# A list of expert items made before a block barrier, and one tile's routing results made after it

## The chip, the cores and the metric

One NeuronCore of a Trainium2 chip runs the whole kernel; the metric is the device time of one execution in microseconds. Engines in the text: TensorE (PE), its weight loads (PEld), VectorE (DVE), ScalarE (ACT), GpSimd (POOL), SyncE (SP); a trailing q in a profile is an engine's sequencer or queue.

## What is computed

One layer of a hybrid block on 1024 tokens of width 1024, in float32: a normalised input goes through an mLSTM group and a differential-attention group, the two are joined, projected and added to the input, and a mixture of experts follows. Only its routing and its start matter here:

```python
u2 = rms_norm(h, norm2_g)
logits = u2 @ router_w + router_b
top_vals, top_idx = lax.top_k(logits, 4)          # 4 of 32 experts
gates = softmax(top_vals)
# tokens are gathered by expert, in blocks
gu = u2[tok] @ w_gu[e] + b_gu[e]
act = (clip(up) + 1) * gate * sigmoid(1.702 * gate)
h[tok] += (act @ w_down[e] + b_down[e]) * gates
out = rms_norm(h, final_g)
```

## The kernel before

`mix_and_route` (L1314) makes the output projection, the second norm and the routing, tile by tile: 8 tiles of 128 tokens, in pairs. `experts` (L1988) then works through a list of items. An item is one expert with up to 128 of its tokens, or up to 192 (two blocks); the list stands in `k.items`: expert, first slot and a flag for two blocks, 64 entries each, and at the end the count. Each of the two functions is one `nc.Block`, one program for each engine; at the end of a block all five engines meet at a barrier. Order within a block is written out by hand, with semaphores.

**Routing of a tile** on DVE (`pair`, L1760, and `slots`, L1701): logits plus bias, top 8, their indices, one-hot rows `oh` and their sum `mask`. TensorE's `rank` (L1602) counts for each expert the tokens ahead, with `macc`, the count of earlier tiles. `slots` adds the expert's region (`base`), adds the token numbers of expert 0 into `first` (128x192; L1707, L1709), updates `macc` (L1716), and makes the four slot numbers `si` (L1717 to L1721). The weights of a tile, softmax numerators by their sum, go with the token number into `pair_of` (L1801 to L1806), and `gates_by_expert` (L1724) spreads them for the bias of the output. GpSimd's `scatter_pairs` (L1886) writes a tile's four columns of pairs (token, weight) at its slots into `slot_table` in DRAM, by four indirect DMAs.

**The last tile** ends the block: DVE makes its weights, `slots`, then copies the row numbers of the first item, summed by TensorE from `first` (L1666), into `first_rows` (L1840, L1841), and makes its gates. GpSimd waits for `first_rows` and gathers the first item's x, 192 rows of `u2_dram` (L1877). Its last scatter stands in the next block (L2108).

**The start of `experts`:**
- DVE: `item_table` (L1915), 19 steps, each with a wait for the one before, on 32 partitions: tokens by expert, blocks beyond the first, running sum over the experts, for each entry the expert, the slot and the flag. Three matmuls of TensorE lie between (`turn_table`, L1973). Then the rest of x (`rest_x`, L2616), `low` of weight chunk 0, two memsets, `low` of chunks 1 and 2, and the items.
- ScalarE: `high` of chunk 0, a table load, the selector of expert 0 (`pick_first`), x's high part (L2470), `high` of chunks 1 to 4.
- TensorE: two table matmuls, the transposes of x (`turn`, L2185) when the gather has landed, the third table matmul, and the items.
- SyncE loads the count (L2082), waits until TensorE has entered the first item, issues two loads for the end of the kernel and then the weight chunks, 1 MB each; chunk n of the running count can be loaded when `low` of chunk n-6 is done.
- GpSimd: the last tile's scatter; when all scatters have landed, the loads of the first item's pairs; two small copies; `fetch(1)` (L2099), the load of the second item's pairs; in the loop over items (L2125) the gather of the second item's x from those pairs (`gather_rows`), and so on.

An item on TensorE (L2283) has twelve weight chunks. Each is split by ScalarE (`high`, L2345) and DVE (`low`, L2488) into a high and a low part, and multiplied in three passes (L2223 to L2225). Between chunks 8 and 9 TensorE transposes the next item's x (`turn_next`, L2190), once it has landed. Every engine starts its loop over items with two loads from `k.items` and an `If` for one or two blocks (L2174):

```python
with eng.Fori(0, count(eng)) as i:
    both = eng.value_load(k.items[0:1, ds(i + 2 * ITEMS, 1)], min_val=0, max_val=1)
    with eng.If(both > 0):
        body(i, 2)
    with eng.Else():
        body(i, 1)
```

Of the kernel before, what the change touches and what calls it, by code (L numbers as in the profile page):

```python
# [7 lines left out]
F32 = mybir.dt.float32  # L8
# [7 lines left out]
P = 128  # L16
# [67 lines left out]
def constants():  # L84
# [16 lines left out]
            "before": (p[:, None] < p[None, :]).astype(f),  # L101
            "expert": np.broadcast_to(np.arange(N_EXPERTS, dtype=f), (P, N_EXPERTS)),
            "region": np.broadcast_to(np.arange(N_EXPERTS, dtype=f) * SEQ, (P, N_EXPERTS)),
            "slot": np.broadcast_to(np.arange(ROWS, dtype=f), (P, ROWS)),
            "token": p[:, None].astype(f),
        },
        "item_consts": {
            "upto": (p[:, None] <= p[None, 0:N_EXPERTS]).astype(f),
            "index": np.broadcast_to(np.arange(ITEMS, dtype=f), (P, ITEMS)),
            "self": p[:, None].astype(f),  # L110
# [1203 lines left out]
def mix_and_route(nc, k):  # L1314
# [42 lines left out]
    k.item_steps, k.item_mm = k.sem("items_chain"), k.sem("items_mm")  # L1357
    k.scattered, k.slot_ready = scattered, slot_ready
    PER = 2 * 15 + 1
# [4 lines left out]
    with ExitStack() as c:  # L1364
# [31 lines left out]
        e4 = sb("e4", [P, TOP_K])  # L1396
        es = sb("es", [P, 2])
        oh = sb("oh", [P, TOP_K, N_EXPERTS])
        ohb = sb("ohb", [P, TOP_K, N_EXPERTS])
        mask = sb("mask", [P, N_EXPERTS])  # L1400
        macc, si, pair_of = k.macc, k.si, k.pair_of
        at_slot = sb("at_slot", [P, ROWS])
        first = sb("first", [P, ROWS])
        tokp = sb("tokp", [P, 1])
        base = sb("base", [P, 1, N_EXPERTS])
        sf = sb("sf", [P, TOP_K])
        tokf = sb("tokf", [P, 1])
# [10 lines left out]
        def begins(i, p):  # L1418
            return isinstance(i, int) and i == 0 and p == 0
# [15 lines left out]
        def _(sp):  # L1435
# [29 lines left out]
            sp.dma_start(k.item_cons[:, :], k.d["item_consts"]).then_inc(small_loaded.sem, 16)  # L1465
# [38 lines left out]
        def _(act):  # L1504
# [54 lines left out]
            def pair(i):  # L1559
                for p in two:  # L1560
# [8 lines left out]
                    if begins(i, p):  # L1569
                        act.wait_ge(rows_stored.sem, rows_stored.at(4, 0))  # L1570
# [21 lines left out]
        def _(pe):  # L1592
# [15 lines left out]
            def pair(i):  # L1608
                for p in two:
# [11 lines left out]
                    if not begins(i, p) and not ends(i, p):  # L1621
                        rank(i, p)
# [42 lines left out]
            pe.wait_ge(k.item_steps, FIRST_MADE)  # L1665
            pe.matmul(l_ps[:, 0:1], first[:, 0:P], k.c["ones"][:, 0:1], start=True, stop=True)  # L1666
            pe.matmul(l_ps[0:HALF_ROWS, 1:2], first[:, P:], k.c["ones"][:, 0:1], start=True, stop=True).then_inc(k.item_mm, 1)

        @block.vector
        def _(dve):  # L1670
# [15 lines left out]
            def tables():  # L1686
                dve.wait_ge(tables_loaded.sem, 16)
                dve.tensor_copy(tokf[:, :], k.c["token"]).then_inc(blanks.sem, 1)
# [12 lines left out]
            def slots(i, p, b, last=False):  # L1701
# [3 lines left out]
                dve.wait_ge(chain, step.next())  # L1705

# [1105 lines left out]
```

## Time and profile before

| | |
|---|---|
| time, median of 3 runs | 2212.57 us (2211.31 to 2213.67) |
| profiled execution, its own time | 2208.72 us |
| its span, first to last instruction | 2206.7 us |
| mean granted TensorE clock | 0.979 |
| busy: PE, PEld, DVE, ACT, POOL | 2135.9, 1813.9, 1712.8, 1373.6, 412.0 us |
| weight chunks of the experts | 426 loads of 1 MB, median 6.5 us to landing |
| HBM read and written | 253 GB/s over the span |

An engine's busy time says how much it has to do, not whether it is waited for; the lines that the argument needs are those of the time between 600 and 700 us, where routing ends and the experts begin. In a line of the timeline the number in brackets is the idle time of the engine ahead of the instruction, with what the trace takes to have ended it. A clock of 1.00 stands for 2.4 GHz, 0.50 for 1.2 GHz.

### The profile page before, as it was taken

To read this page: it belongs to the slowest core of one execution; us is meant where nothing else is said; L and a number is where in the kernel's file an instruction comes from. 1 tells how busy PE (TensorE), PEld (TensorE's weight loads), DVE (VectorE), ACT (ScalarE), POOL (GpSimd) and SP (SyncE) were. 2 spreads that over 40 slices of the span, in tenths; PEclk is the share of its full clock that TensorE was granted. 3 is DMA by queue.
4 is the path that set the end of the run, shared out by engine and by line. 5 is a ranking of instruction groups with operands and counts; after the bars stand their busy time and mean duration, and the time that the engine had idled before them with its cause. 6 is when DMAs were issued, how large, how long until landed. Compare 5 with 4: busy or idle time off the path is not lost. (4 is left out here: it accounts for less than half of the span.)

```text
span 2206.7 us, 35945 instructions
## 1 busy us (share of the span) xinstructions
PE 2135.9 (97%) x11234; PEld 1813.9 (82%) x11235; DVE 1712.8 (78%) x2154; ACT 1373.6 (62%) x1752; POOL 412.0 (19%) x436
## 2 busy tenths in 40 slices
PE   8999999988969999999999999999999999999998
PEld 7987777767858998898898898988889998889884
DVE  5426667776778777979979978779997778998897
ACT  4324655543446656757857757567775667777675
POOL 0000000002342221213212213212321222221121
PEclk9999999998979999999999999999999999999996
DMA  4110101206859667979979979669997769998797
GB/s 162 44 48 34 58 33 45 101 31 221 206 190 343 237 243 253 377 267 349 374 263 351 372 262 353 233 241 380 379 379 267 250 230 327 394 367 335 290 374 281
DMA packets 106798, 548.74 MB, mean 249 GB/s; under 512 B 17877, under 2 KB 28758, under 8 KB 51834
## 3 DMA queue, kind: packets, MB, share of 16 engines
q1 hardware_dynamic: 88138, 504.94, 60.8%
q0 software_dynamic: 18608, 43.12, 8.1%
q8 instruction: 31, 0.51, 0.1%
q14 instruction: 21, 0.17, 0.0%
HBM read 516.49 MB, written 41.47 MB: 253 GB/s over the span
## 5 line engine op out<-in xcount | busy, mean ns | idle before, releaser
L2492 DVE TENSOR_TENSOR wl<-raw,wh 128x2048 fp32r<-128x2048 f32 x423 | 958.6, 2285 | 43.4 <-PE sums L2241 27.0
L2349 ACT ACTIVATE wh<-raw 128x2048 fp32r<-128x2048 f32 x425 | 805.2, 1913 | 128.1 <-DMA raw<-in_w_experts 47.6
L2225 PE MATMUL sums<-wh,xx 128*128 128x512 f32 x832 | 325.6, 391 | 0.0
L2224 PE MATMUL sums<-wl,xx 128*128 128x512 f32 x832 | 325.3, 391 | 0.0
L2223 PE MATMUL sums<-wh,xx 128*128 128x512 f32 x832 | 324.8, 390 | 0.0
L2156 POOL DMA_INDIRECT h_dram<-y,pairs_mine x47 | 121.0, 2574 | 769.7 <-DVE y L2586 453.7
L2223 PE MATMUL sums<-wh,al 128*128 128x512 f32 x560 | 227.0, 405 | 0.5 <-DVE al L2577 0.3
L2225 PE MATMUL sums<-wh,ah 128*128 128x512 f32 x560 | 219.3, 392 | 0.0
L2224 PE MATMUL sums<-wl,ah 128*128 128x512 f32 x560 | 218.7, 390 | 0.0
L2224 PEld LDWEIGHTS sums<-wl,xx 128*128 128x128 f32 x832 | 156.5, 188 | 33.9
L2225 PEld LDWEIGHTS sums<-wh,xx 128*128 128x128 f32 x832 | 156.5, 188 | 33.1
L2223 PEld LDWEIGHTS sums<-wh,xx 128*128 128x128 f32 x832 | 156.9, 189 | 31.1
L2269 PE MATMUL sums<-xx,wh 128*128 128x384 f32 x576 | 172.2, 364 | 0.0
L2270 PE MATMUL sums<-xx,wl 128*128 128x192 f32 x576 | 144.9, 251 | 0.0
L2225 PEld LDWEIGHTS sums<-wh,ah 128*128 128x128 f32 x560 | 105.1, 188 | 23.0
L2223 PEld LDWEIGHTS sums<-wh,al 128*128 128x128 f32 x560 | 105.3, 188 | 21.9 <-DVE al L2577 3.2
L2224 PEld LDWEIGHTS sums<-wl,ah 128*128 128x128 f32 x560 | 105.6, 189 | 18.9
L133 PE MATMUL unit_ps<-u_high,wc_l 128*128 128x512 f32 x288 | 118.5, 411 | 0.9 <-PEq L217 0.9
L2400 ACT ACTIVATE tg<-tg 128x256 f32<-128x256 f32 (+2 forms) x140 | 64.6, 461 | 86.1 <-DVE tg L2511 69.8
L2269 PE MATMUL a_ps<-xx,wh 128*128 128x384 f32 x384 | 114.4, 363 | 0.0
L135 PE MATMUL unit_ps<-u_high,wc_h 128*128 128x512 f32 x288 | 112.9, 392 | 0.0
L134 PE MATMUL unit_ps<-u_low,wc_h 128*128 128x512 f32 x288 | 112.5, 391 | 0.0
(414 smaller groups left out, 4193.5 us busy)
## 6 DMA issues: line engine op xcount, KB each, us to landing
raw<-in_w_experts SPq DMA_DIRECT2D x426, 1024.0 KB, 6.5
raw<-in_w_chan SPq DMA_DIRECT2D x20, 512.0 KB, 3.3
o_gate<-in_x SPq DMA_DIRECT2D x8, 512.0 KB, 5.1
raw<-in_w_out SPq DMA_DIRECT2D x8, 512.0 KB, 5.0
ht<-in_x SPq DMA_DIRECT2D x8, 512.0 KB, 5.2
h_dram<-ht SPq DMA_DIRECT2D x8, 512.0 KB, 5.9
u_dram<-ut SPq DMA_DIRECT2D x8, 512.0 KB, 6.5
h_all<-h_dram SPq DMA_DIRECT2D x8, 512.0 KB, 7.0
```

Of the source, the lines that this page charges most:

```text
L133: pe.matmul(out, ll, rh, start=start, stop=False)
L134: pe.matmul(out, lh, rl, start=False, stop=False)
L135: return pe.matmul(out, lh, rh, start=False, stop=stop)
L2156: pool.indirect_dma_start(out=k.h_dram, out_offset=bass.IndirectOffsetOnAxis(ap=mine[rows, b, 0:1].bitcast(U32), axis=0), in_=y[rows, b, : ...
L2223: pe.matmul(out, lo[:, n, :], w_hi[:, kk, :], start=g >= 4 and n == 0, stop=False)
L2224: pe.matmul(out, hi[:, n, :], w_lo[:, kk, :], start=False, stop=False)
L2225: last = pe.matmul(out, hi[:, n, :], w_hi[:, kk, :], start=False, stop=half == 1 and kk == 3)
L2269: pe.matmul(out[:, 0:2 * ROWS], w_hi[:, kk, own], xx[:, n, :], start=n == 0, stop=False)
L2270: last = pe.matmul(out[:, 0:ROWS], w_lo[:, kk, own], xx[:, n, 0:ROWS], start=False, stop=n == KT - 1)
L2349: nc.scalar.activation(wh[ch % HIGHS][:, :, :], raw[ch % RAW][:, :, :], ACT.Copy).then_inc(h_split.sem, 1)
L2400: nc.scalar.activation(t, t, ACT.Silu, scale=ALPHA).then_inc(sig_ready.sem, 1)
L2492: dve.tensor_tensor(wl[ch % LOWS][:, :, :], raw[ch % RAW][:, :, :], wh[ch % HIGHS][:, :, :], ALU.subtract).then_inc(l_split.sem, 1)
```

## The change

1. The list of items is made at the end of `mix_and_route`, ahead of the barrier. Steps that don't depend on each other share a wait, and some constants come as tables instead of being computed, so eleven values of its semaphore are left where there were 19 steps. The sum of the first rows is taken between two of its steps. No engine waits for the list in `experts` any more.
2. `slots` is cut in three: `places` (base and `macc`), `hold_first` (token numbers of expert 0, now in `held`), and the slot numbers. In a tile of the loop `hold_first` comes after the residual, ahead of the logits; the copy of a tile's base number into `tokp` moves behind the index search, and its waits go.
3. The last tile's weights, slots and gates are no longer made in `mix_and_route`. `last_pairs` makes them in `experts` on DVE, behind the first x's rest and the two memsets, ahead of `low` of chunk 1. GpSimd's last scatter waits for its slots there.
4. In `experts`, `low` of chunk 0 comes ahead of x's rest, `pick` with a loaded expert number takes the place of `pick_first`, and the activation table is loaded behind x's copy. The scratch `hh` becomes part of `av0` and `tg`, with one more wait on DVE in `clamp_rows`. Some small tensors move to another place.

```diff
@@ mix_and_route, DVE: a tile
-                    if not begins(i, p):
+                    if not first(i, p):
+                        places(i, p)
                         slots(i, p, 1 - p)
...
+                    if not first(i, p):
+                        hold_first().then_inc(chain, 1)
+                        step.next()
                     dve.wait_ge(logits.sem, logits.at(i, p + 1))
...
+                    if ends(i, p):
+                        continue
                     dve.wait_ge(e_ready.sem, e_ready.at(i, p + 1))
...
@@ mix_and_route, DVE: the end
-            slots(NT // 2, 0, 1, last=True)
-            dve.wait_ge(k.item_mm, 1)
-            dve.tensor_copy(k.first_rows[0:HALF_ROWS, 1:2], l_ps[0:HALF_ROWS, 1:2])
-            dve.tensor_copy(k.first_rows[:, 0:1], l_ps[:, 0:1]).then_inc(k.item_steps, 1)
-            gates_by_expert(NT - 1, 1)
+            places(NT // 2, 0).then_inc(items, 1)
+            hold_first().then_inc(items, 1)
...
+            dve.wait_ge(item_mm, 1)
+            dve.tensor_copy(it[:, 0:1], l_ps[0:E, 0:1]).then_inc(items, 1)
+            dve.wait_ge(items, made.next())
+            dve.tensor_scalar(it[:, 8:7 + MOST], k.c["past"][0:E, :], it[:, 0:1], None, ALU.is_lt).then_inc(items, 1)
...
+            dve.wait_ge(item_mm, 2)
+            dve.tensor_copy(k.first_rows[0:HALF_ROWS, 1:2], r_ps[0:HALF_ROWS, 1:2])
+            dve.tensor_copy(k.first_rows[:, 0:1], r_ps[:, 0:1]).then_inc(items, 1)
...
+            dve.wait_ge(item_mm, 3)
+            dve.tensor_scalar(it[:, 6:7], own, l_ps[0:E, 2:3], 1.0, ALU.add, ALU.add)
...
+            dve.wait_ge(item_mm, 4)
+            dve.tensor_copy(k.items[:, :], t_ps[0:1, 0:2, :].rearrange("p a b -> p (a b)")[:, 0:3 * ITEMS + 1]).then_inc(items, 1)
@@ new
+def last_pairs(dve, k, ohb, sf):
...
+    dve.wait_ge(k.e_ready.sem, k.e_ready.at(i, p + 1))
+    dve.reciprocal(k.es[:, 1:2], k.es[:, 0:1]).then_inc(chain, 1)
...
+    for n in range(TOP_K):
+        dve.tensor_scalar(gate[:, n, :], k.e4[:, n:n + 1], k.es[:, 1:2], None, ALU.mult)
+        dve.tensor_copy(pair_of[:, n, 0:1], k.tokf[:, :])
+    dve.tensor_tensor(ohb, oh[:, :, :], base[:, :, :].broadcast_to([P, TOP_K, E]), ALU.mult).then_inc(chain, 1)
+    dve.wait_ge(chain, step.next())
+    dve.tensor_reduce(sf, ohb, X, ALU.add).then_inc(chain, 1)
+    dve.wait_ge(chain, step.next())
+    dve.tensor_copy(k.si[p][:, :], sf).then_inc(k.slot_ready.sem, 1)
...
+    dve.tensor_tensor(ohb, oh[:, :, :], gate.broadcast_to([P, TOP_K, E]), ALU.mult).then_inc(chain, 1)
...
@@ experts: SyncE, GpSimd, TensorE, ScalarE, DVE
-            sp.wait_ge(*table_made)
-            pool.wait_ge(*table_made)
...
-            turn_table(pe, k, it, iv, table_l, table_r, 0)
-            turn_table(pe, k, it, iv, table_l, table_r, 1)
+            pe.wait_ge(pairs_kept.sem, pairs_kept.at(0, 0))
             pe.wait_ge(xg_loaded[0].sem, xg_loaded[0].at(0, 16))
             turn(0)
-            turn_table(pe, k, it, iv, table_l, table_r, 2)
-            pe.wait_ge(pairs_kept.sem, pairs_kept.at(0, 0))
-            pe.wait_ge(*table_made)
             per_item(pe, item)
...
+            high(0, 0)
+            pick(0)
             act.sem_inc(y_read.sem, y_read.credit)
-            high(0, 0)
-            nc.scalar.preload_act_table(ACT.Silu)
-            pick_first()
             act.wait_ge(x_turned.sem, x_turned.at(0, 0))
             copy_x(0).then_inc(x_high.sem, 1)
+            nc.scalar.preload_act_table(ACT.Silu)
...
-            item_table(dve, k, it, iv, iw, table_l, table_r)
+            low(0, 0)
             dve.wait_ge(x_high.sem, x_high.at(0, 0))
             rest_x(0).then_inc(x_low.sem, 1)
-            low(0, 0)
             dve.memset(tg[H:, 256:], 0.0)
             dve.memset(uc[H:, 256:], 0.0)
+            last_pairs(dve, k, y[:, 1, 512:512 + TOP_K * N_EXPERTS].rearrange("p (a b) -> p a b", b=N_EXPERTS), y[:, 1, 0:TOP_K])
             for ch in range(1, LOWS - 1):
                 low(0, ch)
```

## Rows read from the trace of the kernel before

**Rows 1.** By stretches: us, busy us by engine (instructions), clock, DMA share, GB/s.
```profile
650.33:2158.00 1507.67, 1505.97 (x7732) 1298.03 (x7733) 1269.16 (x1272) 1037.19 (x1082) 347.35 (x364) 1.00 0.86 315
```

**Rows 2.** Timeline of PE at the seam: start, us, instruction, idle before.
```profile
638.52 1.97 PE L2187 MATMUL x_ps<-cons,mx 128*128 128x128 f32 x8 [1.61 <-DMA mx<-u_dram,first_rows]
...
650.33 0.79 PE L2211 MATMUL sums<-bias,sel 128*128 128x512 f32 x1 [9.12 <-POOL pairs_next L2120]
```

**Rows 3.** TensorE's sequencer, by line: duration ns min/median/max.
```profile
L2065 PEldq TENSOR_LOAD <-items x1: 493/493/493, 641.8 to 641.8; - x1
L2177 PEldq COMPARE_BRANCH  x47: 77/174/3455, 643.6 to 2129.2; - x47
```

**Rows 4.** DMA packets by queue from 647.5 to 648 us: number, MB.
```profile
q8 instruction: 1, 0.02, 14.8%
```

**Rows 5.** Timeline of DVE: the last tile's tail in routing.
```profile
629.11 0.15 DVE L1801 RECIPROCAL es<-es 128x1 f32<-128x1 f32 x1
...
631.59 0.28 DVE L1717 TENSOR_TENSOR ohb<-oh,base 128x128 f32<-128x128 f32 x1
...
632.23 0.17 DVE L1721 CAST si<-sf 128x4 int32<-128x4 f32 x1
...
632.70 0.14 DVE L1841 CAST first_rows<-l_ps 128x1 int32<-128x1 f32 x1
```

**Rows 6.** Timeline of DVE: list of items, x's rest, three low parts.
```profile
634.87 0.07 DVE L1920 MEMSET y<- 32x16 f32 x1 [1.43 <-PEq L1364]
...
641.32 0.35 DVE L1969 CAST items<-a_ps 1x193 int32<-1x193 f32 x1 [0.97 <-PE a_ps L1984]
641.71 1.22 DVE L2497 TENSOR_TENSOR xx<-x_ps,xx 128x1024 fp32r<-128x1024 f32 x1
...
645.80 6.69 DVE L2492 TENSOR_TENSOR wl<-raw,wh 128x2048 fp32r<-128x2048 f32 x3
```

**Rows 7.** Timeline of GpSimd: the chain to the second item's x.
```profile
636.57 1.03 POOL L1892 DMA_INDIRECT slot_table<-pair,si  x1 [0.17 <-issue]
...
640.49 0.97 POOL L1892 DMA_INDIRECT slot_table<-pair,si  x1 [0.30 <-issue]
643.46 0.59 POOL L2112 DMA_DIRECT2D pairs<-slot_table  x1 [2.00 <-issue]
...
651.96 0.54 POOL L2102 DMA_DIRECT2D pairs<-slot_table  x1 [1.62 <-issue]
...
658.68 1.09 POOL L1900 DMA_INDIRECT mx<-u_dram,pairs  x1 [5.60 <-DMA pairs<-slot_table]
```

**Rows 8.** Timeline of DVE (first line) and GpSimd: side by side.
```profile
659.12 2.28 DVE L2492 TENSOR_TENSOR wl<-raw,wh 128x2048 fp32r<-128x2048 f32 x1
...
648.08 2.25 POOL L2120 COPY pairs_next<-pairs 64x2 int32<-64x2 int32 x1
...
660.08 2.18 POOL L1900 DMA_INDIRECT mx<-u_dram,pairs  x1 [0.30 <-issue]
```

**Rows 9.** DMA issues at 640, 600, 651 and 658 us: us to landing.
```profile
slot_table<-pair,si POOLq DMA_INDIRECT x2, 2.6
...
slot_table<-pair,si POOLq DMA_INDIRECT x4, 6.7
...
pairs<-slot_table POOLq DMA_DIRECT2D x1, 0.5 KB, 5.9
...
mx<-u_dram,pairs POOLq DMA_INDIRECT x1, 9.3
```

**Rows 10.** Timeline of PE at the second item's x.
```profile
678.14 1.03 PE L2187 MATMUL x_ps<-cons,mx 128*128 128x128 f32 x8
```

**Rows 11.** By stretches, as rows 1: clock after 650.33, clock at the end.
```profile
653.00:654.00 1.00, 1.00 (x5) 0.76 (x4) 0.00 (x0) 0.00 (x0) 0.08 (x1) 0.76 1.04 434
...
2172.00:2176.00 4.00, 4.00 (x6) 1.50 (x5) 0.00 (x0) 0.00 (x0) 0.72 (x1) 0.55 0.73 109
```

**Rows 12.** Timeline of DVE in a middle tile of routing.
```profile
590.86 0.19 DVE L1776 TENSOR_TENSOR lg<-l_ps,rb 128x32 f32<-128x32 f32 x1 [0.38 <-PE l_ps L1648]
```

More of the change, by code:

```diff
@@ L1416, in is_last, with first @@
             return isinstance(i, int) and i == LAST
-        def begins(i, p):
+        def first(i, p):
             return isinstance(i, int) and i == 0 and p == 0
@@ L1620, in pair @@
                             last.then_inc(half_pe, 1)
-                    if not begins(i, p) and not ends(i, p):
+                    if not first(i, p) and not ends(i, p):
                         rank(i, p)
@@ L1699, in low, with places @@
                 dve.tensor_tensor(ml[p][:, :, :], mx[p][:, :, :], mh[p][:, :, :], ALU.subtract).then_inc(m_low.sem, 1)
-            def slots(i, p, b, last=False):
+            def places(i, p):
                 dve.wait_ge(earlier.sem, earlier.at(i, p))
@@ L1705, in slots, with hold_first @@
                 dve.wait_ge(chain, step.next())
-                dve.tensor_scalar(at_slot[:, :], k.c["slot"], base[:, 0, 0:1], mask[:, 0:1], ALU.is_equal, ALU.mult).then_inc(chain, 1)
+                return dve.tensor_tensor(macc[:, :], macc[:, :], mask[:, :], ALU.add)
+            def hold_first():
+                dve.tensor_scalar(at_slot[:, :], k.c["index"], base[:, 0, 0:1], mask[:, 0:1], ALU.is_equal, ALU.mult).then_inc(chain, 1)
                 dve.wait_ge(chain, step.next())
-                ins = dve.scalar_tensor_tensor(out=first[:, :], in0=at_slot[:, :], scalar=tokp[:, 0:1], in1=first[:, :],
-                                               op0=ALU.mult, op1=ALU.add)
-                if last:
-                    ins.then_inc(k.item_steps, FIRST_MADE)
-                else:
-                    ins.then_inc(chain, 1)
-                    step.next()
-                dve.tensor_tensor(macc[:, :], macc[:, :], mask[:, :], ALU.add)
+                return dve.scalar_tensor_tensor(out=held[:, :], in0=at_slot[:, :], scalar=tokp[:, 0:1], in1=held[:, :],
+                                                op0=ALU.mult, op1=ALU.add)
+            def slots(i, p, b):
                 dve.tensor_tensor(ohb[:, :, :], oh[:, :, :], base[:, :, :].broadcast_to([P, TOP_K, E]), ALU.mult).then_inc(chain, 1)
@@ new lines, in _ @@
+            dve.wait_ge(items, made.next())
+            dve.scalar_tensor_tensor(out=a, in0=index, scalar=it[:, 6:7], in1=a, op0=ALU.is_lt, op1=ALU.mult)
+            dve.tensor_scalar(b, r, -1.0, it[:, 0:1], ALU.mult, ALU.add).then_inc(items, 1)
+            dve.wait_ge(items, made.next())
+            dve.tensor_scalar(v[0], a, own, None, ALU.mult)
+            dve.scalar_tensor_tensor(out=v[1], in0=r, scalar=region, in1=a, op0=ALU.add, op1=ALU.mult)
+            dve.scalar_tensor_tensor(out=few, in0=b, scalar=float(P + HALF_ROWS), in1=a, op0=ALU.is_le, op1=ALU.mult).then_inc(items, 1)
```

205 lines of the change are left out of this document (87 added, 118 removed).

## Prediction

> **What bounds the kernel now.** I read the granted clock and span first, then the chain of work that ended last; it reaches back only over the last 28 us, all biases and the final norm, and says nothing of the places that this change touches. So I took the busy time by stretches. From 650.33 us to 2158 us TensorE is busy 1505.97 of 1507.67 us at full clock [rows 1]: the experts' loop is TensorE's own, and whatever moves the loop's start, or opens a gap in it, moves the end by as much. What the change can touch is the seam between routing and that loop. TensorE's timeline shows it: the transposes of the first x start at 638.52, the first product only at 650.33 after 9.12 us of idle time [rows 2]. The trace names a GpSimd copy as the releaser; the semaphore that TensorE waits for on the pair copies had been high enough long before, so I don't believe it. TensorE's sequencer tells more: it loads the item count at 641.8, as soon as the list of items is there, and its first branch of the per-item `If`, at 643.6, takes 3455 ns, where the median of all 47 is 174 ns [rows 3]. It is over at 647.1, every semaphore that the first product needs has fired by then, and still the product starts 3.2 us later; in that stretch the only packet on any queue in its half microsecond is one of instructions [rows 4]. I read both as code being fetched at a first visit. So now the loop's start hangs on: list of items ready (641.67), 2.0 us of register loads, 3.5 us branch, 3.2 us second fetch.
>
> **The list of items, in fewer stages and before the barrier.** Its DVE chain runs from 634.87 to 641.67 [rows 6], 6.8 us in 19 waited steps. The change makes it in about ten, and starts it while the first rows are still summed. Gathering x must not wait longer: the row numbers are ready at 632.84 [rows 5]. In the new order the running count is added ahead of the held rows (+0.1), the copy of the tile's base number is put between two top-8 steps (+0.1), and four short list steps run while TensorE sums the held rows. I put it at 632.84 + 0.1 to 0.2, so x lands at about 638.7 instead of 638.5. What is left of the list after that: one matmul turn, five waited DVE steps, another turn, the cast. By the old durations (6.8 us for 19 steps, three turns in them) some 3.6 us: the list is ready at about 636.6. At the low end it is free, at the high end it takes its old 6.8 us (639.7). The barrier between the blocks comes after it, at 636.9 instead of 634.4. Who is late for that: ScalarE's first weight copy (1.9 us by the page of the profile, to 638.9) and the expert's selector behind it (639.3), both before it needs x (640.6): nothing. DVE's first low part, 2.28 us, from 638.9 to 641.2, now ahead of x's rest: it ends before the 641.7 at which the rest starts today [rows 6]: nothing.
>
> **TensorE's start.** Its sequencer no longer waits for the list after the transposes are issued. The count is loaded when those have been issued, say 0.8 us after x lands: 639.5 instead of 641.8, 2.3 us earlier. x's rest ends at 642.9, inside the branch. With the same two fetches the first product is at 648.0. Bounds: 650.3 if the fetches are held up by something else, 643.1 (right behind x's rest) if none of them is paid. I take 648.0, since both fetches belong to a first visit and move with it.
>
> **Routing's loop.** The held rows go behind the residual and in front of the logits. In a middle tile DVE waits 0.38 us there for the logits [rows 12], and the two instructions take 0.8, so the logits' sum starts up to 0.5 us late, but its result is needed by TensorE only after the next 24 products; and two waited steps are gone at the tile's end. I cost it at nothing; if that cover were gone, 0.5 us for each of 7 tiles, in the range.
>
> **The last tile's weights, slots and gates, moved.** They leave routing's tail, where the weights (from 629.11) hid beside the rank matmuls and where slots (to 632.40) and gates hid beside the row numbers (632.84) [rows 5]. That frees the tail of almost nothing. Where they go, DVE first has to end x's rest (641.71 + 1.22 = 642.93) and two memsets (0.54): 643.5. Weights from 629.11 to about 630.1 are 1.0 us, slots from 631.59 to 632.40 are 0.8: the slots are ready at 645.3 instead of 632.40, the gates, a product and a sum like those of the slots, some 0.7 us later. DVE's next three low parts then run 646.0 to 652.7 without a gap, as they do now from 645.80 [rows 6]; TensorE needs the second of them about 4.6 us after its start, at 652.6: nothing.
>
> But GpSimd hangs on the slots. Now it starts the last tile's four scatters at 636.57, starts the last of them at 640.49, loads the first pairs at 643.46 when all have landed, the next item's pairs at 651.96, and issues the gather of the **second item's x** at 658.68 [rows 7]; that takes 9.3 us to land [rows 9]: 668.0. TensorE turns this x behind the ninth chunk, at 678.14 [rows 10]. So there are 10 us of cover today. Moved, the chain is:
> - first scatter at 645.3 + 0.8 = 646.1 (a shift of 9.5 us, nearly all the cover);
> - each scatter takes 1.0 us and 0.3 between them today. Now they fall among DVE's low parts. In the trace a GpSimd gather that began at 660.08, inside a low part that ran to 661.40, took 2.18 us and ended 0.86 behind it; its like that began before that part took 1.09 [rows 8]. So three of the four end 0.85 us behind a low part: the last at 653.5 (650.9 without such waits, 655.9 if all four wait);
> - landing 1.6 us behind that where the queues are empty (2.6 from issue), 5.7 where they are full (6.7) [rows 9]. SyncE starts the seventh weight chunk at about 648, so they are full: I take 5.0, 658.5;
> - 0.6 to the pair loads, 0.6 for the second, 5.9 to land under load [rows 9]: 665.6; the two copies (0.3 if DVE is quiet; one took 2.25 beside a low part [rows 8]) 0.7: 666.3; 1.6 to the next fetch, and then 6.7 to the gather as now (651.96 to 658.68): 674.6;
> - gather: 9.3 as now, 8 if the weights' stream thins out while TensorE stands: 682.6.
>
> TensorE wants it at 648.0 + 27.8 = 675.8. It stands for 6.8 us, and turns x at 682.6 instead of 678.14: **+4.5 us**. From here on nothing depends on when the loop began. A pause of that length also costs clock: at the end of the kernel TensorE stood for under 3 us and the granted clock fell from 1.0 to 0.55 in the stretch that followed, and after 650.33 it came back only within 653 to 654 [rows 11]. Products at 1.2 GHz take twice the time, so some 3 us of them are 1.5 us lost. Sum: 4.5 + 1.5 = **+6.0 us**.
>
> A rule that speaks against one term: the Trainium skill, SBUF — State Buffer, section "SBUF: two separate sides", has DVE and GpSimd share a port pair under an exclusive lock, and a tensor_tensor with two SBUF inputs blocks only GpSimd's reads; and the page's section "Who interferes with whom" infers from this that the writing of descriptors goes on beside a tensor_tensor. By that inference the four scatters would run at their 1.0 us. The trace's gather of 2.18 us, whose end trails the low part's by 0.86, goes against it here. That case is the second rival.
>
> **Other edits.** The scratch `hh` becomes part of two tiles that exist; the one new DVE wait, for the item before to have read its sums, stands behind a wait for later products: nothing. Final weights and biases of the norm are issued by SyncE when TensorE enters its body, as now: nothing.
>
> **Rivals.**
> 1. The pair chain is in time (queues nearly empty: scatters landed at 652 to 655, gather issued at 666, landed by 675.8). Then only the earlier start shows: -2.3 us, and 2210.2. For it: each transfer has a quiet row; against it: the weights' stream begins at the same moment.
> 2. Scatters not held by DVE's low parts: the chain is 2.6 us shorter, x turned at 680.0, +1.9, clock +1.3: 2215.8.
> 3. Slower still: all four scatters held, both copies too, and the gather at the 12 us and more that a loaded queue can cost: x at about 689, +11 with the clock: 2224. It decides where the weights' stream fills every queue from 648 on.
> 4. The change doesn't bring TensorE's start forward (650.3 again), because the fetch and not the list sets it. That alone gives 2212.6; with the late pair chain it gives the same time as the forecast, since x of the second item sets the end in both.
> 5. Faster: the fetches run beside x's landing and the product starts at 643 to 645, and the chain loses the copies' 3 us beside the low parts as well: x turned at 674, 2208.5.
>
> **How the numbers follow.** The profiled execution took 2208.72 us, 2.0 more than its span of 2206.7; the median of the runs is 2212.57. I add the sum to the median: 2212.57 + 6.0 = 2218.6. Chances: forecast 0.55 (2215.5 to 2221.5), rival 1 0.17, rival 2 0.13, rival 3 0.08, rival 5 0.07. A measurement of this kernel can tell 0.2% (4.4 us) from no change: slower is over 2217.0, faster under 2208.1. The forecast lies above 2217.0 for some 0.46 of its 0.55, rival 3 wholly; rival 2 and most of rival 1 within; so slower 0.55, same 0.38, faster 0.07. The range reaches from rival 1 to near rival 3: 2210.5 to 2223.5.
>
> **What would show it.** In the changed kernel: the list's cast before the barrier, at about 636.5; the first product at about 648; the last tile's slots at about 645.3; the four scatters with two or three of them near 2 us; the second item's gather issued near 674; TensorE idle for 4 to 9 us at the turn of the second item's x, with a DMA as releaser, and half clock behind it. Wrong would be: no gap at that turn (then rival 1 or 5), scatters of 1.0 us (rival 2), or idle time elsewhere in the loop.

## Result, and the profile after

The changed kernel takes 2216.65 us (median; 2211.80 to 2219.04) beside 2209.28 us for the kernel before (2203.87 to 2213.67): ratio 1.0034, 95% interval 1.0024 to 1.0044, some 7.4 us slower. The forecast was 2218.6 us with a sum of +6.0. The changed kernel's profiled execution took 2216.41 us, and its span is 7.7 us longer than that of before (2206.7 us). From the page of the changed kernel: the span, busy time by engine, and the queue that fetches instructions (packets, MB).

```profile
span 2214.4 us, 35969 instructions
...
PE 2134.0 (96%) x11236; PEld 1810.6 (82%) x11237; DVE 1709.4 (77%) x2142; ACT 1374.6 (62%) x1752; POOL 397.5 (18%) x436
...
q8 instruction: 34, 0.56, 0.1%
```

TensorE has no more work than before (2134.0 us busy against 2135.9), so the time went into waits. TensorE's timeline (start, duration, instruction; in brackets the idle time before it), against [rows 2, 10]:

```profile
638.59 1.94 PE L2182 MATMUL x_ps<-cons,mx 128*128 128x128 f32 x8 [2.37 <-DMA mx<-u_dram,first_rows]
644.33 0.76 PE L2206 MATMUL sums<-bias,sel 128*128 128x512 f32 x1 [3.80 <-issue]
...
685.70 1.97 PE L2182 MATMUL x_ps<-cons,mx 128*128 128x128 f32 x8 [12.06 <-DMA mx<-u_dram,pairs]
...
757.86 1.09 PE L2182 MATMUL x_ps<-cons,mx 128*128 128x128 f32 x8 [2.79 <-issue]
```

The first x is turned where it was (638.59; lines in between left out), the first product comes 6.0 us sooner (644.33), and then TensorE stands 12.06 us for the second item's x, which it turns at 685.70 instead of 678.14. A second pause of 2.79 us, released by nothing that the trace shows, lies at 757.86. DVE, against [rows 5, 6]: list (636.33), slots (645.09), the low parts of chunks 1 to 4 in one line.

```profile
636.33 0.35 DVE L1892 CAST items<-t_ps 1x193 int32<-1x193 f32 x1 [0.96 <-PE t_ps L1675]
...
645.09 0.17 DVE L1963 CAST si<-y 128x4 int32<-128x4 f32 x1
...
646.04 8.90 DVE L2478 TENSOR_TENSOR wl<-raw,wh 128x2048 fp32r<-128x2048 f32 x4
```

GpSimd, against [rows 7]: the four scatters, the first pair load, the copy, the next item's fetch, the gather of the second x, and the copy that comes once it has landed.

```profile
646.11 3.13 POOL L1942 DMA_INDIRECT slot_table<-pair,si  x1 [8.73 <-DVE si L1963]
649.54 1.85 POOL L1942 DMA_INDIRECT slot_table<-pair,si  x1 [0.31 <-issue]
651.70 1.88 POOL L1942 DMA_INDIRECT slot_table<-pair,si  x1 [0.30 <-issue]
653.88 1.90 POOL L1942 DMA_INDIRECT slot_table<-pair,si  x1 [0.30 <-issue]
662.32 0.59 POOL L2108 DMA_DIRECT2D pairs<-slot_table  x1 [6.54 <-issue]
...
668.90 0.18 POOL L2115 COPY pairs_next<-pairs 128x2 int32<-128x2 int32 x1 [4.84 <-DMA pairs<-slot_table]
...
671.05 0.54 POOL L2098 DMA_DIRECT2D pairs<-slot_table  x1 [1.60 <-issue]
...
675.99 2.62 POOL L1974 DMA_INDIRECT mx<-u_dram,pairs  x1 [3.81 <-DMA pairs<-slot_table]
...
686.22 0.18 POOL L2138 COPY pairs_next<-pairs 128x2 int32<-128x2 int32 x1 [5.51 <-DMA mx<-u_dram,pairs]
```

Here is the late chain. In a GpSimd row the time is how long GpSimd is busy with the instruction, not how long the transfer takes. All four scatters run beside DVE's low parts and take 3.13, 1.85, 1.88 and 1.90 us instead of 1.0. Between the end of the last (655.78) and the first pair load lie 6.5 us, 2.0 before. The clock by stretches (last three numbers: granted clock, DMA share, GB/s), against [rows 11]:

```profile
644.33:650.40 6.07, 6.07 (x14) 4.78 (x15) 5.90 (x10) 6.07 (x5) 3.98 (x2) 0.50 0.60 219
...
684.00:691.40 7.40, 5.70 (x18) 4.84 (x19) 0.00 (x0) 1.02 (x1) 1.45 (x4) 0.50 0.06 18
```

From 644.33 to 650.40 TensorE works at 1.2 GHz, and again from 685.70 to 691.3, behind the stall.

### The profile page after: what moved, and what is told of

It reads as the page before. It is cut to its first block and busy times, and to the rows that moved or that the text cites. A ratio compares the mean times of both kernels' runs of the same rounds, so it can differ in the third digit from the quotient of the medians.

```text
span 2214.4 us, 35969 instructions
## 1 busy us (share of the span) xinstructions
PE 2134.0 (96%) x11236; PEld 1810.6 (82%) x11237; DVE 1709.4 (77%) x2142; ACT 1374.6 (62%) x1752; POOL 397.5 (18%) x436
## 5 line engine op out<-in xcount | busy, mean ns | idle before, releaser
L2478 DVE TENSOR_TENSOR wl<-raw,wh 128x2048 fp32r<-128x2048 f32 x423 | 958.9, 2286 | 45.7 <-PE sums L2236 29.4
```

Of the source, the lines that this page charges most:

```text
L2478: dve.tensor_tensor(wl[ch % LOWS][:, :, :], raw[ch % RAW][:, :, :], wh[ch % HIGHS][:, :, :], ALU.subtract).then_inc(l_split.sem, 1)
```

## Experiments

Routing, whose code the variants below hardly touch, ends at different times in different executions: in the profiles the first x is turned between 633.7 and 639.1 us. So places are given relative to that turn (x1), in us. "Second x" is the start of the second item's turn, "rest" is the time from there to the end of the span. "Chain" is the time from the end of the last scatter to GpSimd's first copy behind the landing of the second x. Ratios are to the kernel before, run beside each. e7, e8, e10 and e12 are built on e1.

Everything but the ratio comes from one profiled execution of each kernel, and single executions of one kernel lie up to 10 us apart. The profiled one of e10, for instance, is the slowest of its eleven (2209.15 us, median 2203.24), that of e12 the fastest of its eleven (2200.29, median 2203.97). So a difference of a few us in "rest" counts only where rows say what it is made of.

| kernel | ratio (95%) | first product | second x | rest | last scatter ends | chain |
|---|---|---|---|---|---|---|
| before | 1 | x1 + 11.8 | x1 + 39.6 | 1528.6 | x1 + 2.9 | 28.6 |
| changed | 1.0034 (1.0024 to 1.0044) | 5.7 | 47.1 | 1528.7 | 17.2 | 30.4 |
| e1 slots first | 1.0021 (1.0009 to 1.0032) | 5.7 | 44.8 | 1529.9 | 9.4 | 37.3 |
| e2 start held | 1.0028 (1.0017 to 1.0039) | 17.8 | 47.0 | 1531.1 | 16.2 | 24.2 |
| e3 slots later | 1.0083 (1.0060 to 1.0107) | 6.0 | 50.4 | 1536.0 | 21.1 | 29.8 |
| e4 slots in routing | 1.0006 (0.9992 to 1.0019) | 6.4 | 37.0 | 1529.4 | 7.1 | 31.8 |
| e7 stream behind scatters | 0.9989 (0.9980 to 0.9998) | 5.9 | 37.9 | 1528.0 | 9.4 | 27.8 |
| e8 stream behind pairs | 1.0010 (1.0000 to 1.0020) | 6.1 | 40.2 | 1527.3 | 9.4 | 28.5 |
| e9 changed, stream held | 1.0025 (1.0015 to 1.0035) | 5.9 | 46.7 | 1526.2 | 17.2 | 27.7 |
| e10 chunks behind scatters | 0.9991 (0.9981 to 1.0001) | 6.1 | 35.4 | 1532.6 | 9.4 | 28.3 |
| e5 scratch alone | 0.9996 (0.9985 to 1.0007) | 12.3 | 41.2 | 1525.9 | 3.1 | 29.4 |
| e11 before, 4 on | 1.0005 (0.9993 to 1.0017) | 9.3 | 37.8 | 1529.6 | 2.8 | 30.8 |
| e12 e10, 64 on | 0.9991 (0.9982 to 1.0000) | 6.0 | 36.9 | 1523.5 | 9.4 | 29.7 |
| e13 tiles moved | 0.9989 (0.9978 to 1.0001) | 11.7 | 40.1 | 1523.4 | 2.6 | 29.0 |

### Where the slots stand, and when TensorE starts

**e1**: `last_pairs` ahead of the first low part.

```diff
+            last_pairs(dve, k, ...)
             low(0, 0)
...
             dve.memset(uc[H:, 256:], 0.0)
-            last_pairs(dve, k, ...)
```

> The changed kernel with one move: the last tile's weights, slots and gates are the first thing that DVE does in the experts' block, ahead of the first low part, instead of behind x's rest and the two memsets. In the changed kernel DVE idles from 637.2 to 639.2 there, so the move should cost DVE under 1 us. Theory (the late chain slots, scatters, pairs, gather of the second x sets the end): slots ready at about 639.2 instead of 645.2, the four scatters over by 646 instead of 655.8, the second item's x turned at 673.7 to 677 instead of 685.7, TensorE idle there 0 to 3 us instead of 12; time 0.9945 to 0.996 of the changed kernel, and 1.5 to 4.5 us below the kernel before. Rival (the loss comes with the list's new place or with how TensorE's code lies in its pages, not with the slots): the idle time at the second x goes, but the time stays 6 to 8 us above the kernel before.

**e2**: TensorE held behind the turn of the first x.

```diff
             turn(0)
+            pe.wait_ge(*low_done(0, 2))
             per_item(pe, item)
```

> The changed kernel, in which TensorE waits behind the turn of the first x until DVE's third low part is done (some 650.4 us by the changed kernel's trace), so that the first product starts where it did in the kernel before, 6 us later than in the changed kernel. Theory (the second item's x, turned at 685.7, sets the end whatever the start): time within 2 us of the changed kernel, and the idle time at the second x is about 6 us instead of 12.1. Rival (the loop's start carries through to the end): 5 to 6 us slower than the changed kernel, and 12 us of idle time stay.

**e3**: `last_pairs` behind `low` of chunks 1 and 2.

> The changed kernel with the last tile's weights, slots and gates behind DVE's second and third low part (2.28 us each) instead of ahead of them. Theory (the chain from the slots sets the end, one for one): slots 4.5 us later; the four scatters meet one low part fewer, which gives back up to 2 us; the second x is turned 2.5 to 4.5 us later than 685.7, idle there 14.5 to 16.5 us, time 3 to 4.5 us above the changed kernel. Rival (the queues under the weight stream set when the second x lands, not the slots): the second x at 685.7 as before, time the same.

**e4**: `last_pairs` called in `mix_and_route`, behind the cast of the list.

> The changed kernel with the third part undone: the last tile's weights, slots and gates are made in the routing block, at its end behind the cast of the list of items, about 2 us before the barrier (barrier at about 639 instead of 637.2); the list in fewer stages stays. Theory: slots ready at about 638.7, scatters from 639.5, second x turned at 674 to 678, idle there under 3 us; but ScalarE's first weight copy starts 2 us later, so the first product may start at 645 to 647; time 0.995 to 0.997 of the changed kernel, 0 to 3.5 us below the kernel before. Rival (the early list or the code's place costs by itself): time stays 6 to 8 us above the kernel before although the idle time at the second x is gone.

Measured: e2 is no slower than the changed kernel, although its first product comes 12 us later relative to x1 (the wait held it 6 us longer than meant). So the earlier start is worth nothing there, and the rival falls. The theory had some 6 us of idle time left at the second x; e2 has none, since no bracket stands behind its turn, and that is a first sign that the chain itself had become shorter (24.2 us, 30.4 in the changed kernel):

```profile
651.48 0.77 PE L2206 MATMUL sums<-bias,sel 128*128 128x512 f32 x1 [15.86 <-issue]
...
680.67 1.04 PE L2182 MATMUL x_ps<-cons,mx 128*128 128x128 f32 x8
```

e3 moved the second x by the 3.3 us expected, but the time by more, some 10.8 us over the changed kernel (0.0049 of 2206; both intervals together leave some 6 us either way). 7.3 us of it lie behind the second x; five waits for `av` that its trace shows there, 3.4 us together, are part of that, and the rest is open.

e4 undoes the third part: second x at x1 + 37.0, ratio down to 1.0006. So the third part costs the time. What is left of the change (the early list, the earlier start, the small tensors in their new places) is together within 0.2% of the kernel before.

e1 is the surprise. The slots are ready at 636.41, 0.6 us behind x1, and the last scatter is over 7.8 us sooner than in the changed kernel, yet the second x comes only 2.3 us sooner and TensorE stands almost as long:

```profile
680.63 1.97 PE L2182 MATMUL x_ps<-cons,mx 128*128 128x128 f32 x8 [10.74 <-DMA mx<-u_dram,pairs]
```

My theory had a stall of 0 to 3 us. GpSimd in e1:

```profile
637.26 3.12 POOL L1942 DMA_INDIRECT slot_table<-pair,si  x1 [2.86 <-DVE si L1963]
...
643.25 1.94 POOL L1942 DMA_INDIRECT slot_table<-pair,si  x1 [0.30 <-issue]
652.71 0.59 POOL L2108 DMA_DIRECT2D pairs<-slot_table  x1 [7.52 <-issue]
...
659.48 0.21 POOL L2115 COPY pairs_next<-pairs 128x2 int32<-128x2 int32 x1 [5.04 <-DMA pairs<-slot_table]
...
669.19 3.14 POOL L1974 DMA_INDIRECT mx<-u_dram,pairs  x1 [4.58 <-DMA pairs<-slot_table]
...
682.53 0.19 POOL L2138 COPY pairs_next<-pairs 128x2 int32<-128x2 int32 x1 [7.12 <-DMA mx<-u_dram,pairs]
```

The scatters are over at 645.19, and the first pair load goes out 7.5 us later, where it took 2.0 before [rows 7] and 1.8 in e2; the pairs then take 6.8 us to the copy. The DMA share by stretches suggests why (e7 tests it): in e1 the queues are at work from 641 on, and full while the scatters have to land,

```profile
640.00:644.00 4.00, 2.52 (x6) 2.09 (x7) 3.10 (x4) 3.99 (x4) 3.08 (x4) 0.50 0.44 145
...
648.00:652.00 4.00, 4.00 (x20) 3.30 (x19) 3.62 (x4) 2.94 (x2) 0.00 (x0) 1.00 1.02 410
```

and in the changed kernel from 645 on:

```profile
640.00:644.00 4.00, 0.53 (x3) 0.13 (x1) 3.69 (x8) 3.40 (x3) 0.00 (x0) 0.50 0.02 4
...
648.00:652.00 4.00, 4.00 (x14) 3.17 (x13) 4.00 (x3) 4.00 (x3) 3.39 (x3) 0.70 0.87 317
```

### The weight stream starts with TensorE

SyncE's first loads in the experts' block wait for TensorE's entry into the first item. Changed kernel (first) and kernel before:

```profile
644.05 0.34 SPq L2081 DMA_DIRECT2D final_g<-in_final_g  x1
...
647.23 30.92 SPq L2075 DMA_DIRECT2D raw<-in_w_experts  x12
```

```profile
647.32 0.34 SPq L2085 DMA_DIRECT2D final_g<-in_final_g  x1
...
650.45 38.59 SPq L2078 DMA_DIRECT2D raw<-in_w_experts  x14
```

The final weights and the biases are issued 0.3 us ahead of the first product in the changed kernel (644.05), and the weight chunks follow. In the kernel before that was 647.32, 3.9 us behind the first pair load [rows 7]. So the change, which starts TensorE sooner, also starts 3.3 us sooner the stream that fills all queues, and the chain of small transfers that the second x needs then runs inside it. e7, built on e1, tests that:

```diff
             sp.wait_ge(x_turned.sem, x_turned.at(0, 1))
+            for p in range(2):
+                sp.wait_ge(k.scattered[p].sem, k.scattered[p].at(NT // 2, 0))
             sp.dma_start(k.final_g[:, :], ...)
```

> The kernel of e1_slots_first, in which SyncE waits, before its first load in the experts' block (final weights, biases, then the weight chunks), until the last tile's scatters have landed. In e1 that stream begins at 641.2, 5.4 us behind the turn of the first x, and the scatters, over at 645.2, take 7.5 us until the pair loads are issued, where they take 2.0 in the kernel before, whose stream begins at 647.3. Theory (the stream, which begins with TensorE's first item, slows the chain of small transfers from 34 us to 41): the pair loads are issued 2 us behind the last scatter, the second x is turned 34 to 36 us behind the first instead of 44.8 (before: 39.6), idle there under 2 us, time 8 to 10 us below e1 and 3 to 5 below the kernel before. Rival (the chain's length comes from DVE's low parts and from the slots, not from the stream): the second x still 43 us or more behind the first, time as e1.

**e8**: the same as e7, with a wait for the first pairs (`idx_loaded`) behind it.

> As e7, but SyncE waits until the first item's pairs have landed too, some 3.5 us longer. Theory: the pairs land 1 to 2 us sooner, but the seventh weight chunk now lands later than TensorE wants it (22 to 24 us behind the first x against 20.5), so TensorE idles 1.5 to 4 us inside the first item, and the second x is turned 35.5 to 38 us behind the first: 0 to 2 us slower than e7. Rival (weights have more slack than that): no idle time inside the first item, and time as e7 or up to 1 us below.

**e9**: the changed kernel with e7's wait, the slots where the change put them.

> The changed kernel, its slots left where they are (6.6 us behind the turn of the first x), with the one wait of e7: SyncE's stream waits until the last tile's scatters have landed, about 19 us behind the first x instead of 5.5. Theory: from the last scatter to the second x 24 us (as in e2_start_held) instead of 30: the second x is turned 41 to 42 us behind the first instead of 47.1, TensorE's idle time is split between a late seventh weight chunk (3 to 8 us) and the second x (the rest up to 7), time 5 to 6 us below the changed kernel and 0 to 3 above the kernel before. Rival (the slots' own lateness, 8.7 us, is the whole cause): the second x still 46 to 48 us behind the first, time as the changed kernel.

**e10**: e7, but with its wait between the biases and the weight chunks.

> As e7_stream_after_scatters, but only the weight chunks wait for the scatters; the final weights and the output biases (some 0.6 MB) are issued before that wait, as in e1. In e7 TensorE idles 2.8 us inside the first item, since the seventh chunk was issued only at 649.7, 2.2 us behind the end of SyncE's wait. Theory (that chunk sets this idle time): the chunk is issued 2 us earlier, the idle time there falls to about 1 us, the second x is turned 36 to 38 us behind the first (e7: 37.9), time 0 to 2 us below e7. Rival (the small chain, slowed by the 0.6 MB beside the scatters, sets the second x): the pair loads are issued 1 to 3 us later than in e7 and the second x is turned 38 to 40 us behind the first.

Measured: e7 stands at 0.9989 (0.9980 to 0.9998), some 7 us below e1 and 10 below the changed kernel by ratio, and 2.4 below the kernel before. This last step is no gain of the early list: e7 also has the changed kernel's places of the tiles, and these alone give 0.9989 (e13 below). SyncE, GpSimd and TensorE in e7:

```profile
649.71 39.38 SPq L2075 DMA_DIRECT2D raw<-in_w_experts  x15
```

```profile
644.33 1.93 POOL L1942 DMA_INDIRECT slot_table<-pair,si  x1 [0.30 <-issue]
648.05 0.60 POOL L2110 DMA_DIRECT2D pairs<-slot_table  x1 [1.79 <-issue]
...
652.81 0.18 POOL L2117 COPY pairs_next<-pairs 128x2 int32<-128x2 int32 x1 [3.03 <-DMA pairs<-slot_table]
...
661.26 1.45 POOL L1974 DMA_INDIRECT mx<-u_dram,pairs  x1 [5.43 <-DMA pairs<-slot_table]
...
674.09 0.19 POOL L2140 COPY pairs_next<-pairs 128x2 int32<-128x2 int32 x1 [6.22 <-DMA mx<-u_dram,pairs]
```

```profile
642.79 0.76 PE L2208 MATMUL sums<-bias,sel 128*128 128x512 f32 x1 [3.98 <-issue]
...
659.67 0.44 PE L2196 MATMUL a_ps<-cons,av 128*128 128x128 f32 x2 [2.84 <-DVE av L2555]
...
674.77 1.03 PE L2184 MATMUL x_ps<-cons,mx 128*128 128x128 f32 x8
```

The last scatter ends at 646.26, the pair load follows after 1.8 us instead of e1's 7.5, the pairs reach the copy in 4.8 instead of 6.8, and the chain is 27.8 us long instead of 37.3: 9.5 us for one wait of SyncE. Some 7.7 of them are the landing of the scatters and the first pairs; 2.1 are two GpSimd copies of which one, in e1, happened to fall beside a low part (2.26 us at 659.63); the steps behind them take 0.3 us more in e7. The second x is turned without a stall, at x1 + 37.9 instead of 44.8. The theory is confirmed in its mechanism, but it gave more: the second x at x1 + 34 to 36, and 8 to 10 us below e1 where 7 were measured. The row at 659.67 shows what is late next, 2.84 us for `av`. In e9 the same wait of TensorE (for `av`) is 9.40 us long, and ScalarE's timeline names its cause:

```profile
661.49 1.91 ACT L2342 ACTIVATE wh<-raw 128x2048 fp32r<-128x2048 f32 x1 [12.87 <-DMA raw<-in_w_experts]
663.30 0.40 ACT L2389 ACTIVATE tg<-tg 128x256 f32<-128x256 f32 x1
```

ScalarE stands 12.87 us for the seventh weight chunk, and the work that TensorE needs is queued behind that copy on ScalarE. So the stream may be held for some microseconds only. e8 holds the stream 3 us longer, stalls 3.51 us there, and is slower than e7, as its theory said, though by more (some 4.6 us by ratio, 0 to 2 expected; second x at x1 + 40.2, not 35.5 to 38). e9's second x at x1 + 46.7 and its time (1.0025 against 1.0034, intervals that overlap) are what its rival had. But it comes there without a wait at the second x: the chain is shorter than in the changed kernel, though only in part (27.7 us, not 24), and TensorE lost to the late chunk what it would have won. So e9 decides nothing between the two. In e10 the stall at that `av` is 0.15 us and the second x comes at x1 + 35.4, which decides for its theory, but its time is e7's (0.9991); the 2.5 us don't show.

### What stands inside the loop

Behind the second x the changed kernel takes as long as the kernel before (1528.7 and 1528.6), though it loses time there to the low clock and to the pause at 757.86. Something gives it back. The sequencer's branch of the `If`, against [rows 3], and the large products of the two-block items before and after:

```profile
L2172 PEldq COMPARE_BRANCH  x47: 77/208/5302, 640.4 to 2136.5; - x47
```

```profile
L2269 PE MATMUL sums<-xx,wh 128*128 128x384 f32 x576 | 172.2, 364 | 0.0
```

```profile
L2264 PE MATMUL sums<-xx,wh 128*128 128x384 f32 x576 | 170.3, 361 | 0.0
```

One branch, at 751.0, took 5.30 us, the first, at 640.4, took 3.4, and 34 packets of instructions were fetched, 31 before. The products of 384 columns take 361 instead of 364 ns, and two-block items are 0.42 us shorter: from turn to turn 57.2 instead of 57.6 us (the expectations say 57.6 and 58.0; the difference is the same). Four runs take these apart.

**e5**: on the kernel before, the scratch alone.

```diff
-        hh = sb("hh", [H, 512])
+        hh, out_hh = av[0][0:H, :], tg[0:H, :]
...
+                if g == 0:
+                    dve.wait_ge(y_read.sem, y_read.at(i, 0))
```

> The kernel before with only the edit of the scratch `hh` (it becomes part of two tiles that exist, with the one new wait of DVE), for the 10 us that the two-block items give back in the changed kernel. Theory (the scratch has nothing to do with it, since the operands of these products lie at the same addresses in both kernels): two-block items as long as before, time within 2 us of the kernel before. Rival (the new layout or the new wait is what shortens them): each of some twelve two-block items 0.4 us or more shorter, time 4 to 6 us below the kernel before.

**e11**: on the kernel before, at the head of TensorE's first block:

```diff
+            for _ in range(4):
+                pe.sem_inc(k.passed, 1)
```

> The kernel before with nothing but 4 semaphore increments at the head of TensorE's program, where it waits for its first input; they put the experts' loop of TensorE 4 instructions further into the program, where the changed kernel has it. Two differences of the changed kernel are in question: its two-block items take 57.6 us instead of 58.0 (some 13 of them), and its fetches of code (no second pause of 3.2 us before the first product, but one of 3 us at about 750). Theory (both hang on where the code lies, not on the change): items of 57.6 us; first product 8.5 to 9 us behind the first x instead of 11.8; a pause of 3 us near 745; time 3 to 6 us below the kernel before. Rival (they come from the change itself): all three as in the kernel before, time the same within 1.5 us.

**e12**: e10 with 64 of them.

> e10 with 64 semaphore increments at the head of TensorE's program, which put its code 64 instructions further on. Theory (the pause of 3 us at about 745 comes with where a branch of the loop and its target lie): the pause goes or moves, two-block items stay at 57.6 us, time 0 to 3 us below e10. Rival (the pause comes with the first item of that kind, wherever the code lies): a pause of 3 us there as in e10, time the same.

**e13**: on the kernel before, the shared tiles laid as in the changed kernel (constants, `macc`, `si`, `pair`, `first_rows` behind `bias`, a filler of 32 columns ahead of the raw weights).

> The kernel before, its instructions unchanged, with the tiles that the routing and the experts share laid in SBUF as in the changed kernel: the constants and the small tiles behind `bias` instead of ahead of the raw weights, two fillers in their place, so that the raw weights, `bias`, the gates and the gathered x lie at the changed kernel's addresses. In question are the 0.4 us by which each two-block item is shorter in the changed kernel (57.6 against 58.0 us, some 13 items), which neither the scratch nor the place of TensorE's code gave. Theory (it is the layout): 57.6 us for these items, the products of line 2269 at a mean of 361 instead of 364 ns, time 3 to 6 us below the kernel before. Rival (something else in the change): 58.0 us and 364 ns, time the same within 1.5 us.

Measured: e5 leaves the items at 57.6 us and the time the same; it is not the scratch. e11 settles the fetches: with 4 instructions in front, the kernel before shows the changed kernel's pauses,

```profile
645.20 0.77 PE L2214 MATMUL sums<-bias,sel 128*128 128x512 f32 x1 [6.61 <-issue]
...
743.61 1.09 PE L2190 MATMUL x_ps<-cons,mx 128*128 128x128 f32 x8 [2.84 <-issue]
```

the first product 9.3 us behind the first x instead of 11.8, and 2.84 us lost at 743.61; its products stay at 364 ns and its time is the same, one pause for the other. Every kernel here built on the changed one shows a pause of 2.6 to 3.8 us at that place, except e12; the kernel before, e5 and e13 show none. So 2.5 of the 6.0 us by which the first product came sooner are no merit of the list, and the later pause is no fault of it: both hang on where the code lies. e12 has no such late pause in its trace (its longest branch takes 3.6 us, e10's 6.3), yet its time is e10's (0.9991 both, 0.001 either way): the 3 us don't show in the times. e13 settles the products:

```profile
L2269 PE MATMUL sums<-xx,wh 128*128 128x384 f32 x576 | 170.3, 361 | 0.0
```

361 ns, with not one instruction changed. Two turns of x in the kernel before and in e13 show it for one item, 43.13 us against 42.71:

```profile
687.47 1.03 PE L2187 MATMUL x_ps<-cons,mx 128*128 128x128 f32 x8
...
730.60 1.04 PE L2187 MATMUL x_ps<-cons,mx 128*128 128x128 f32 x8
```

```profile
683.72 1.03 PE L2187 MATMUL x_ps<-cons,mx 128*128 128x128 f32 x8
...
726.43 1.04 PE L2187 MATMUL x_ps<-cons,mx 128*128 128x128 f32 x8
```

Nine of the twelve two-block items have it, three stay at 43.1: 3.8 us in all. The rest is 1523.4 us instead of 1528.6, 5.2 less, but 1.9 of these are two places, at 1049 and 1251 us, where TensorE waits 0.55 and 0.67 us for `av` in the profile of the kernel before and the turns of x lie 1.0 and 0.9 us further apart. The profiles of e5 and e11, with the old layout, don't have them either, so they don't come from the layout. By time e13 is at 0.9989 (0.9978 to 1.0001), 2.4 us with 2.5 either way: the 3.8 lie within that, and so does nothing at all, if only just. Which of the moved tiles does it, and by what, wasn't tried, nor why three items don't have it.

With that the 7.7 us between the two profiles can be accounted for: second x +7.5 relative to x1 and x1 itself +0.1. Behind it the distances between the turns of x differ by +2.7 for the low clock (12.0 us from the second x to the third instead of 9.3), +2.9 for the late fetch, -3.8 for the layout and -2.0 for the two items that wait in the profile of the kernel before; some +0.3 are spread over the rest. Sum +0.1, measured +0.1. These are two executions, so the terms that come from waits (the -2.0 above all) are not a cost of either kernel.

## Why the prediction was right, and where it was not

- **List and barrier.** Forecast: cast at 636.6, first x at 638.7. Measured 636.33 and 638.59. Right.
- **TensorE's start.** Forecast 648.0, measured 644.33. The step that failed is "both fetches belong to a first visit and move with it": the branch at 640.4 kept its 3.4 us, the second pause went, because TensorE's code lies elsewhere (4 instructions in front do the same to the kernel before, e11). It cost the forecast nothing, as rival 4 said that the start and the end are decoupled by the late chain, and e2 showed it.
- **Slots.** 645.3 forecast, 645.26 measured, first scatter at 646.1 and 646.11.
- **Scatters.** Three held by the low parts, last one over at 653.5; all four were held, 655.78, the upper bound that the text gave (655.9). The second rival had them at 1.0 us. The second and third scatter of e1, whose start lies outside a low part, take 0.98 and 0.97 us. The Trainium skill, SBUF — State Buffer, section "Who interferes with whom", infers that descriptors are written on beside a tensor_tensor. The four rows of 1.85 to 3.13 us, each ending 0.84 to 0.92 us behind the end of a low part, speak against that for these scatters; what of a scatter is held, its reading of the slots in SBUF or its writing, no run here tells.
- **Landing and pairs.** From the last scatter's end to the pair load 5.6 us put, 6.5 measured. From there to the end of the copies 7.2 put, 7.1 measured. From fetch to gather 6.7 put, 4.9 measured. From gather to the turn 8 put, 9.7 measured. So x came at 685.70 and not 682.6, 3.1 us later: +2.3 from the scatters' time on GpSimd, +0.9, -0.1, -1.8 and +1.7 from these.
- **Stall and clock.** 6.8 us of idle time forecast, 12.06 measured: TensorE was ready 2.2 us sooner (673.6, not 675.8), which has no weight at the end, and x came 3.1 later. The clock fell to 0.50, as was forecast in kind, and cost 2.7 us where 1.5 was put.
- **The sum.** +4.5 and +1.5 were forecast; +7.5 and +2.7 came. What kept the total near the forecast is none of its terms: in the two profiles the tiles' new places gave back 3.8 us, waits that only the profile of the kernel before has 2.0, and a fetch took 2.9. So the mechanism (the pair chain becomes the bound) was right, the size of its terms too small by some 4 us together, and the total right partly by luck. The premise that behind the second x nothing but the clock changes was wrong by some 2.6 us, in the kernel's favour.
- **The base.** The forecast added its +6.0 to 2212.57 us, the median of three runs; that of twelve is 2209.28. On this base it would have read 2215.3, so the absolute time was met partly because a base 3.3 us too high made up for a sum too small. The measured 2216.65 also lies just under the 2217.0 that the text wanted for "slower", although the ratio's interval is clear of 1.
- **What the text did not see.** It said that the weights' stream fills the queues from 648 on and took that as given. It is itself set by TensorE's start (644.05 against 647.32), so the change makes its own collision. Rival 3 had the full queues but not this link. e1 and e7, which differ by one wait of SyncE, show it: 9.5 us of chain, some 7.7 of them in the landing of small transfers.

## What to carry to other kernels

When an engine's earlier start also releases a bulk stream, look at which small transfers used to run in the quiet before it: in e1 the scatters and first pairs took some 7.7 us longer, and one wait on the stream's queue gave that back (e7), while a few microseconds more starved the consumer (e8, e9). Work moved off an engine that had slack (DVE's tail of routing) to behind another step is paid by the longest chain that hangs on its result, not by the engine. And before a difference of some microseconds is put down to an edit, move the code by a few instructions and the tiles by a few hundred bytes: here these two alone made pauses of 2.5 to 2.8 us come and go, and 3.8 us of products. A difference of some microseconds between two profiles has to be found in their rows before it is put down to anything: two waits in one profile were 1.9 us of the 5.2 that the layout seemed to give.

## What the runs showed of the hardware that I had not expected

- Moving the tiles that hold raw weights, biases, gates and the gathered x changes the pace of products that read none of these: 364 to 361 ns in the mean, over 1,152 products of 384 columns, 3.8 us in nine of twelve items (e13 against before). The products' own operands are laid at a fixed boundary by `begin_at` in both kernels; which of the moved tiles matters is open.
- Four instructions ahead of a loop move its first-visit fetches: a pause of 2.5 us before the first product vanished and one of 2.84 us came 98 us later (e11). The Trainium skill, Runtime: NRT & Kernel Launch, section "Instruction fetch mechanics", has a taken branch to code outside the window force a fetch before execution goes on; the 5.30 us branch beside a median of 208 ns agrees for a first visit, and the 34 packets of 0.56 MB in all agree with its blocks of 16 KiB. Later passes through the loop show no such stall.
- From the first product on, the granted clock stayed at 0.50 for 3.2 us in the kernel before, 4.6 in e11, 4.5 in e13 and 5.3 in e5, though these four run the same instructions there, and for 4.2 (e1) to 6.2 us (e2) in the changed kernel and its variants, 6.0 in the changed kernel itself. What sets the length isn't shown; the cost of the slow products is part of every "second x" above.
- A GpSimd scatter that starts less than 0.1 us behind the start of a 2.28 us subtraction of DVE takes 3.12 or 3.13 us, in e1, e2, e7 and the changed kernel alike; e1's third, which starts 0.08 us ahead of one (641.98 against 642.06), takes 0.97.
